# Gate products shared evenly over the heads of a scan, and third weight slabs begun on their high parts

## What is computed

```python
def gla_project(h, w_in, w_a1, w_a2, b_a):
    p = h @ w_in                     # q, k, v and the output gate g
    ...
    logits = jnp.einsum('zbtr,zrk->zbtk', low, w_a2) + b_a[:, None, None, :]
    log_decay = jax.nn.log_sigmoid(logits.astype(jnp.float32)) / GLA_GATE_NORM

def step(state, inp):                # one chunk of tokens
    attn = jnp.einsum('bhtd,bhsd,bhtsd->bhts', qc, kc, jnp.exp(rel))
    out = attn @ vc + jnp.einsum('bhtd,bhdv->bhtv', qc * jnp.exp(cum), state)
    ...

def gla_output(o, g, head_norm, w_out):
    o = from_heads(rms_norm(o, head_norm))
    return (o * jax.nn.silu(g)) @ w_out
```

## Time and profile before

| | us |
|---|---|
| median of 3 runs | 1747.23 (1746.46 to 1747.80) |
| the profiled execution, its run | 1749.78 |
| its span, first to last instruction | 1748.0 |
| TensorE busy in the span | 1671.9 (96%) |
| VectorE busy | 1122.3 (64%) |
| ScalarE busy | 713.5 (41%) |
| scan, gram(0, 0) to head_output(3) | 1140.8 to 1293.0 |

### The profile page before, as it was taken

How to read it: one execution, slowest core, us unless ns; L and a number is a source line. 1 busy time by engine, 2 the same in 40 slices (tenths; PEclk the granted TensorE clock), 3 DMA queues, 4 the chain that set the end, 5 groups by cost and what they waited for, 6 DMA issues and landing times.

```text
span 1748.0 us, 23892 instructions
## 1 busy us (share of the span) xinstructions
PE 1671.9 (96%) x9008; PEld 1398.0 (80%) x9008; DVE 1122.3 (64%) x1816; ACT 713.5 (41%) x1060; POOL 85.9 (5%) x57
## 2 busy tenths in 40 slices
PE   7999999998999999999999899989989899999997
PEld 6888877887888888888888787857677688888885
DVE  6678666477787577864865554187755664464456
ACT  4212565335333223322334663256544543343345
POOL 0200000122000000000002200000002100000002
PEclk9999999999999999999999999999989999999998
DMA  8344100031433334333322112011112233333332
GB/s 355 110 149 157 49 1 1 25 133 39 143 122 121 130 108 144 104 136 133 109 62 85 49 49 61 24 35 37 37 49 84 62 96 95 96 96 97 96 96 73
DMA packets 37280, 159.51 MB, mean 91 GB/s; under 512 B 4145, under 2 KB 4401, under 8 KB 31057
## 3 DMA queue, kind: packets, MB, share of 16 engines
q1 hardware_dynamic: 37202, 158.44, 27.4%
HBM read 156.33 MB, written 2.10 MB: 91 GB/s over the span
## 4 chain that ended last, share of the span: by engine, by line
PE 87%; DVE 5%; ACT 4%; issue 2%; DMA 1%; SPq 0%; POOL 0%; ACTq 0%; DVEq 0%
PE pm L464 65%; PE pm L698 4%; PE pm L874 3%; PE pm L618 2%; PE pm L484 2%; PE pm L644 2%; PE pm L817 2%; PE pm L631 1%; ACT mod_t L959 1%; DMA ada_w<-first_ada 1%; PE pm L799 1%; DVE h_res L1634 1%; PE pm L575 1%; ACT w_hi L940 1%; PE pm L531 1%
## 5 line engine op out<-in xcount | busy, mean ns | idle before, releaser
L1358 DVE TENSOR_TENSOR w_lo<-raw,w_hi 128x1024 fp32r<-128x1024 f32 x185 | 230.4, 1247 | 374.2 <-ACT w_hi L940 371.7
L940 ACT ACTIVATE w_hi<-raw 128x1024 fp32r<-128x1024 f32 x181 | 191.8, 1060 | 638.3 <-PE pm L464 576.1
L464 PE MATMUL pm<-x_hi,w_hi 128*128 128x512 f32 (+1 forms) x1536 | 446.1, 352 | 3.6 <-DVE w_lo L1358 3.6
L464 PE MATMUL pm<-x_hi,w_lo 128*128 128x512 f32 (+1 forms) x1536 | 448.7, 354 | 0.0
L464 PE MATMUL pm<-x_lo,w_hi 128*128 128x512 f32 (+1 forms) x1536 | 444.1, 351 | 0.0
L464 PEld LDWEIGHTS pm<-x_hi,w_hi 128*128 128x128 f32 x1536 | 250.2, 189 | 49.4 <-DVE w_lo L1358 6.0
L464 PEld LDWEIGHTS pm<-x_hi,w_lo 128*128 128x128 f32 x1536 | 248.8, 189 | 39.6
L464 PEld LDWEIGHTS pm<-x_lo,w_hi 128*128 128x128 f32 x1536 | 247.2, 188 | 41.4
L464 PE MATMUL pm<-hid_hi,w_hi 128*128 128x512 f32 (+1 forms) x396 | 119.5, 356 | 1.7 <-DVE w_lo L1358 1.7
L464 PE MATMUL pm<-hid_hi,w_lo 128*128 128x512 f32 (+1 forms) x396 | 120.7, 359 | 0.0
L464 PE MATMUL pm<-hid_lo,w_hi 128*128 128x512 f32 (+1 forms) x396 | 119.3, 355 | 0.0
(11 more groups left out here) (224 smaller groups left out, 2363.2 us busy)
## 6 DMA issues: line engine op xcount, KB each, us to landing
raw<-slabs SPq DMA_DIRECT2D x185, 512.0 KB, 3.6
ada_w<-ada SPq DMA_DIRECT2D x44, 1024.0 KB, 4.9
ada_w<-first_ada SPq DMA_DIRECT2D x4, 1024.0 KB, 19.1
raw<-gates SPq DMA_DIRECT2D x8, 512.0 KB, 3.6
h_res<-x SPq DMA_DIRECT2D x4, 768.0 KB, 17.1
out<-h_res SPq DMA_DIRECT2D x8, 256.0 KB, 2.0
rope<-rope SPq DMA_DIRECT2D x1, 512.0 KB, 23.9
level_f<-level SPq DMA_DIRECT2D x1, 448.0 KB, 3.3
```

Source lines behind the costliest of these rows:

```text
L464: last = pe.matmul(out_p[:, a:b], w[slot][:, ks], x[:, k, a:b], start=(k == 0 and w is w_hi and x is hi), stop=(k == tiles - 1 and w is w_lo))
L940: act.activation(w_hi[nxt % 2][:, :], raw[nxt % 4][:, :], ACT.Copy).then_inc(sem["split_hi"], 1)
L1358: dve.tensor_tensor(w_lo[nxt % 2][:, :], raw[nxt % 4][:, :], w_hi[nxt % 2][:, :].bitcast(FP32), ALU.subtract).then_inc(sem["split_lo"], 1)
```

## The change

**In the scan.** `GATE_STEPS` is written anew: each head does two gate slabs, 16 tiles. Heads 0 to 2 spread them over their seven levels as 3, 3, 2, 3, 2, 2, 1; head 3 does 4, 4, 3, 3, 2 in its first five. `GATE_READY` is the same step as the last tiles, and `copy_gate` moves in ScalarE's step from ahead of the diagonal, the key copies and `level_decay` to behind `level_decay`. The high parts of the first two output slabs move on ScalarE from b = 4 to b = 6 of the last head; their low parts move on VectorE from b = 5 and 6 of the last head to behind its last scan and `output_rms(2)`.

**Third slabs.** `slab_high_first` takes the place of `slab` for slab 2 of each stage, twelve in all: the attention's input and output projections, both up-projections, six down-projections (three groups in each layer), the scan's projections and its output projection. It waits for `split_hi` and `psum_free`, does w_hi x hi and w_hi x lo for all k tiles, then waits for `split_lo` and does w_lo x hi for all.

```diff
-        GATE_STEPS = {0: (0, 0, 5), 1: (0, 5, KT)}
-        for i in range(1, KT):
-            for n, k in enumerate(range(0, KT, 3)):
-                GATE_STEPS[3 * i - 1 + n] = (i, k, min(k + 3, KT))
-        GATE_READY = {s + 1: i for s, (i, _, k) in GATE_STEPS.items() if k == KT}
+        GATE_STEPS = {}
+        for h in range(GLA_HEADS):
+            spans = ((0, 3), (3, 6), (6, 8), (8, 11), (11, 13), (13, 15), (15, 16)) if h < GLA_HEADS - 1 else (
+                (0, 4), (4, 8), (8, 11), (11, 14), (14, 16))
+            for b, (k, end) in enumerate(spans):
+                i = 2 * h + k // KT
+                GATE_STEPS[GLA_LEVELS * h + b] = (i, k % KT, (end - 1) % KT + 1)
+        GATE_READY = {step_: i for step_, (i, _, end) in GATE_STEPS.items() if end == KT}
...
+            def slab_high_first(base, u, hi, lo, tokens, tiles=KT, banks=2):
+
+                s = base + u
+                slot, out_p = s % 2, pm[s % 2] if banks == 2 else pm[u % 4]
+                pe.wait_ge(sem["split_hi"], s + 1)
+                pe.wait_ge(sem["psum_free"], s + 1 - banks)
+                for w, xs in ((w_hi, (hi, lo)), (w_lo, (hi,))):
+                    if w is w_lo:
+                        pe.wait_ge(sem["split_lo"], s + 1)
+                    for k in range(tiles):
+                        for x in xs:
+                            for a, b in HALVES if tokens == TOK else HALVES[:1]:
+                                last = pe.matmul(out_p[:, a:b], w[slot][:, k * P:(k + 1) * P], x[:, k, a:b],
+                                                 start=(k == 0 and w is w_hi and x is hi),
+                                                 stop=(k == tiles - 1 and w is w_lo))
+                last.then_inc(sem["slab_done"], 1)
...
             for s in range(2, 8):
-                slab(0, 0, s, x_hi, x_lo, TOK)
+                (slab_high_first(0, s, x_hi, x_lo, TOK) if s == 2 else slab(0, 0, s, x_hi, x_lo, TOK))
                 head_squares(s - 2)
...
-                    copy_gate(GLA_LEVELS * h + b)
                     if b == 0:
                         diagonal(h)
...
                     level_decay(GLA_LEVELS * h + b + 2)
+                    copy_gate(GLA_LEVELS * h + b)
...
-                    if h == GLA_HEADS - 1 and b == 4:
+                    if h == GLA_HEADS - 1 and b == GLA_LEVELS - 1:
                         for s in range(S_GLA_OUT, S_GLA_OUT + 2):
                             act.wait_ge(sem["gate_done"], KT)
                             split(s, s)
...
-                    if h == GLA_HEADS - 1 and b >= BLOCK_LEVEL:
-                        rest(S_GLA_OUT + b - BLOCK_LEVEL, S_GLA_OUT + b - BLOCK_LEVEL)
             scan(2 * GLA_HEADS - 1)
             output_rms(GLA_HEADS - 2)
+            for s in range(S_GLA_OUT, S_GLA_OUT + 2):
+                rest(s, s)
             scale_output(GLA_HEADS - 2)
```

More of the change, by code:

```diff
@@ L685, in _ @@
             first_slabs(S_ATTN_OUT, x_hi, x_lo, TOK, outs, before=last_units)
-            for u in range(1, KT):
-                if u >= 2:
-                    slab(S_ATTN_OUT, 0, u, x_hi, x_lo, TOK)
+            slab_high_first(S_ATTN_OUT, 2, x_hi, x_lo, TOK)
+            for u in range(3, KT):
+                slab(S_ATTN_OUT, 0, u, x_hi, x_lo, TOK)
             stats(0)
@@ L723, in ffn @@
                         first_modulated(s, 2 * layer, tokens)
-                        for u in range(2, 4):
-                            slab(s, 0, u, x_hi, x_lo, tokens, banks=4)
+                        slab_high_first(s, 2, x_hi, x_lo, tokens, banks=4)
+                        slab(s, 0, 3, x_hi, x_lo, tokens, banks=4)
                     with pe.Fori(1 if g == 0 else 0, tiles // 2) as i:
@@ L730, in ffn @@
                     first_down(s, tokens, tiles, FT * layer + sum(FF_GROUPS[:g]))
-                    for u in range(2, KT):
+                    slab_high_first(s, 2, hid_hi, hid_lo, tokens, tiles, banks=4)
+                    for u in range(3, KT):
                         slab(s, 0, u, hid_hi, hid_lo, tokens, tiles, banks=4)
@@ L755, in _ @@
             for n in range(2 * GLA_HEADS):
-                if n >= 1:
+                if n == 1:
+                    slab_high_first(S_GLA, n + 1, x_hi, x_lo, TOK)
+                elif n > 1:
                     slab(S_GLA, 0, n + 1, x_hi, x_lo, TOK if n < GLA_HEADS else LAT)
@@ L912, in _ @@
                         before=last_head)
-            for u in range(2, KT):
+            slab_high_first(S_GLA_OUT, 2, o_hi2, o_lo2, LAT)
+            for u in range(3, KT):
                 slab(S_GLA_OUT, 0, u, o_hi2, o_lo2, LAT)
```

## The result

| | before | after |
|---|---|---|
| median of the first comparison, us | 1746.65 (6 runs) | 1727.86 (6 runs, 1721.03 to 1739.68) |
| ratio | | 0.9897 [0.9858, 0.9936] |
| all runs of both kernels, those beside the experiments too | 1745.42 (101 runs) | 1732.56 (27 runs) |
| the profiled execution's run and span | 1749.78, 1748.0 | 1732.71, 1730.9 |
| TensorE busy | 1671.9 | 1661.2 (96%) |

The kernel is faster, by 18.8 us in the first comparison and by 12.9 us over all runs; the forecast was 13.2. The two profiles differ by 17.1 us.

The account below looks back on a forecast made before the run. TensorE's queue was taken to bound the scan until VectorE takes over in the last head. 9.0 - 2.6 + 2.8 less 0.7 gave 8.5; with 4.7 from third slabs, 13.2 us less: 1734.0 us, range 1728.5 to 1741.0.

Parts of the forecast that it names:

- Part A: The scan's changes (even gate tiles, early bank copy, moved output splits): 8.5 us less.
- first term: Scan up to where VectorE takes over in the last head: 17.2 us saved less 8.2 of new waits, 9.0 gained.
- term for handovers: Some fourteen more handovers between engines in the scan, 0.05 us each: 0.7 us lost.
- Second term: From VectorE's takeover in the last head to the last gram: 2.6 us lost to gate tiles moved there.
- Third term: From the last gram to head_output(3): TensorE at full clock, 2.8 us gained of 10.4.
- rival (1): Last head: TensorE's clock falls all the same, the stretch behind the last gram stays 10.4 us; 1736.8 us, chance 0.20.
- Part B: Third slabs starting on high parts: 1.6 us at three two-bank places, 3.1 at five four-bank ones, 4.7 in all.
- the twelve more: Possible extra EventSemaphore instructions at the third slabs' waits, 51 ns each, 0.6 us; the forecast kept zero.
- (2): VectorE and ScalarE bound the scan's even heads, TensorE's waits twice 8.2 us; 1742.2 us, chance 0.12.
- (3): More gained: output projection's clock stays behind slab 2's start (1.5 us), scan handovers cost 3.5 us less; 1729.0 us, chance 0.15.
- (4): Third slabs' gain lost again at their w_lo pass or slab 3's split, only Part A stays; 1738.7 us, chance 0.06.
- (5): ScalarE stands at the scan's eight bank copies, exponentials late by 2.5 us each: 6.8 us slower, 1754.0 us, chance 0.04.

Follow-up runs that it names:

- e1: The changed kernel again, unedited; 1730.47 us (12 runs), ratio 0.9935 to the kernel before.
- e10: The changed kernel once more, unedited, beside the kernels with slab 7's tiles placed otherwise; 1732.90 us, ratio 0.9936 to the kernel before.
- e4: The kernel before with only the bank copy moved to the step that fills the bank, old tile table; 1739.44 us, ratio 0.9983.
- e5: New tile table with the bank copied one step later in its old place, old third slabs, output splits as changed; 1732.41 us, ratio 0.994 to before.
- e2: The changed kernel with the old third slabs, so only the scan's changes; 1741.88 us (12 runs), ratio 0.9987 to the kernel before.
- e8: The changed kernel with the first two output slabs' splits back in their old places; 1735.34 us, ratio 0.9959 to the kernel before.
- e3: The changed kernel with the old tile table, bank copy and splits, so only the new third slabs; 1741.34 us, ratio 0.9995 to the kernel before.
- e7: The changed kernel plus three idle products in the last two steps of the last head; 1734.24 us (12 runs), ratio 0.995 to the kernel before.
- e9: The changed kernel with the old table for slabs 0 to 6, slab 7's tiles 3, 3, 2 at b = 0, 3, 4 of the last head; 1729.25 us.
- e12: The changed kernel plus idle products in the last head's last two steps, a second look; 1734.23 us (8 runs), ratio 0.994 to before.
- e6: The changed kernel with the old table for slabs 0 to 6, slab 7's tiles 4 and 4 at b = 3, 4 of the last head; 1731.29 us.
- e11: The 4 and 4 kernel of e6 again, beside the changed kernel; 1730.51 us, ratio 0.9916 to the kernel before.

## Why the prediction was right, and where it was not

**The sum.** 13.2 us was forecast, 13.05 is what the two parts' own stretches gave between the two profiles (8.35 and 4.70), and 12.9 what all runs give. That they agree so well is in part luck: 13.05 holds 2.6 us of clock, of which the two other profiles of this kernel have 1.0, 12.9 holds some of the uneven draw, and within groups the change is worth 9.5 to 12.6. The first comparison's median, 1727.86, is 0.6 us below the low end of the range, with three of its six runs at the faster pace; those of e1 and e10, 1730.47 and 1732.90, lie inside it.

**Part A, first term** (9.0 forecast: 17.2 of work, waits and clock less 8.2 of new waits). From gram(0, 0) to VectorE's o_buf in the last head 123.4 us went to 115.0 (1137.05 to 1252.07): 8.4. The new waits ahead of it are 4.2 us for pairs, 1.6 for sides, 1.6 for the scan's states: 7.4 us. Right, but for one reading: that the 17.2 us need both the even table and the early copy. e4 and e5 show that either does it.

**Second term** (2.6 lost). From o_buf to the last gram 18.3 us went to 20.9 (1252.07 to 1272.99): 2.6. Right. Working through the levels step by step gave these two terms within 0.6 us, and the term for handovers, 0.7, is as large as what the first came out short by. gram(3, 0) came 11.1 us nearer to gram(0, 0), of 12 forecast.

**Third term** (2.8 gained by the clock). Its size was right in after, 2.56 us (10.40 to 7.84), and wrong as a forecast. The step that failed is "so I take the full clock" for one station by itself. e1, e2, e8 and e10 have 9.4 to 9.5 us there, which is rival (1) in part (it said 10.4), and e1, e2, e5 and e10 lost 1.6 us in head_output(3), three of them on top of that, where before lost none. Over such profiles A is worth what its first two terms are, 5.8 us to the last gram (141.7 to 135.9), and what the clock adds or takes behind it changes from execution to execution; A alone measured 4 by the groups.

**Part B** (1.6 and 3.1, 4.7 in all). 1.34 us at the two-bank places, limited by the bank copy as forecast (0.48, 0.29, 0.57 against 0.55, 0.4, 0.65), and 3.36 at the four-bank ones. In the second the starts themselves came 0.45, 0.51, 0.91, 0.62 and 0.64 us sooner, 3.1 in all, as forecast. Two things were left out that nearly cancel: the first matmuls behind a stop are also spaced wider (0.34 and 0.24 us where 0.23 is steady), so where the stop is gone 0.1 to 0.2 us more is gained, 0.8 at the five places; and at the last one 0.5 us is lost again, at the fourth slab. The third slab's own low part was never late: no profile has a wait inside it. The first third slab starts at 52.82 us; with the start-up's 1.27 us that is the forecast's 54.0.

A wait that is met costs nothing that shows: at 1450.05 the slab starts 0.23 us behind the instruction before it, with two waits of its own and one 51 ns EventSemaphore ahead. The Trainium skill ("Perfetto Trace Analysis", Identifying Dependency Chains) speaks of such extra instructions for waits on several engines, and the trace agrees as to where they stand: 12 at `slab_high_first`'s psum_free wait and 63 at `slab`'s, 75 as before. The new wait for the low part, by itself between two matmuls, has none. So the twelve more that the prediction priced at 0.6 us never came, and no run here tests that price.

**Rivals.** (1) The clock falls in the last head all the same: 1.6 of the 2.6 us, in four of six profiles with the new table. (2) VectorE and ScalarE bound the even heads: the waits for VectorE are 7.4 us to the spread, not 16; refuted, though head 0 is VectorE's now. (3) More: its place was right. The output projection lost nothing in after (32.94 us against 34.56), and with B no profile shows a fall behind slab 2's start. Its other half, cheaper handovers, did not come. That B is the cause is likely, not shown, as e2 kept its rate there behind a 1.9 us stop. This coupling is also the one candidate for both parts together giving more than their sum. (4) Only A stays: refuted by e3 against before within groups, and by e1 against e2. But its mechanism is there at one of the eight places, with the sign named for it, a gap ahead of the fourth slab: 0.23 us idle, 0.5 us lost. The argument against it, that two thirds of a slab cover the low part, counted only the third slab. (5) ScalarE stands at the bank copies: it waits 2.6 us in all for gate products, the longest 1.9, and no wait for an exponential is among VectorE's rows of the scan; refuted.

## What to carry to other kernels

A wait on a copied bank can be removed by an earlier copy or by other work ahead of the bank's next use; try the cheaper one alone before both, since here the moved copy gave 7.8 us to the last gram and the rewritten table 5.8. An even share over equal steps is not the goal: a tile costs nothing only where its engine would have waited anyway, and a wait filled at one place returns where the next engine is last. A single profile can hold several us of clock and pace that belong to that execution: hold the same stretch against several profiles before a term is booked.

## What the runs showed of the hardware

- The 768-token slabs ran at one of two paces, 8.32 or 8.48 us for 48 matmuls, at a granted clock of 1.00 in both: for all of 421 to 960 us the same one, 10 us of 1735 apart. In four of fourteen profiles (e5, e7, e9, e12) the stage ahead of that had the other pace. The first stage (384 matmuls in 66.67 us from some 110 us on) has the same pace in all.
- At the end of the scan TensorE's rate fell behind stops of 1.9 to 2.7 us in some executions and not in others (the same kernel: e1 and e10 against after behind 1.97 us, e6 against e11 behind 2.67; behind 1.93 us e5 fell and e2 did not). One fall costs 1.6 us, sometimes 2.9. A short stop is no safety: in after the clock is at 0.50 from 999.1 us on with no stop over 0.92 us in the 9 us ahead.
- Whether the rate falls at one stop says little of the next: six profiles (e1, e2, e3, e6, e7, e10) fell at two or three stops in a row, and both profiles with idle products kept the rate at the first stop and fell at the next.
